# The feed-forward stages of a two-layer block multiply fp32 operands as they are

## The reference, cut to what matters

```
D_MODEL, SEQ, D_FF, CONV_WIDTH = 1024, 256, 2816, 3

def _conv_ffn(h, w_up, conv_w, conv_b, w_down):
    T = h.shape[1]
    u, v = jnp.split(h @ w_up, 2, axis=-1)
    up = jnp.pad(u, ((0, 0), (CONV_WIDTH - 1, 0), (0, 0)))
    uc = conv_b
    for j in range(CONV_WIDTH):
        uc = uc + up[:, j:j + T] * conv_w[j]
    return (jax.nn.silu(uc) * v) @ w_down

# in each layer of the first block:
        x = _layer_norm(ALPHA * x + g1 * y, ln_g[l, 0], ln_b[l, 0])
        h = x * (1.0 + sc2) + sh2
        y = _conv_ffn(h, ffn_w_up[l], ffn_conv_w[l], ffn_conv_b[l], ffn_w_down[l])
        x = _layer_norm(ALPHA * x + g2 * y, ln_g[l, 1], ln_b[l, 1])
```

## Time and profile before

| | us |
|---|---:|
| median of three runs | 4321.88 |
| the profiled execution | 4311.35 |
| its span, first to last instruction | 4309.5 |
| feed-forward part of layer 0, from its modulation to the next layer norm | 212.57 |
| feed-forward part of layer 1, likewise | 212.45 |
| TensorE busy in the whole span | 3165.2 (73%) |

### The profile page before, as it was taken

One profiled execution on the slowest core, in us unless ns is written; L12 is line 12 of the kernel. 1 busy time (PEld: TensorE's weight loads), 2 busy tenths in 40 slices (PEclk: granted clock), 3 DMA queues, 4 the chain that ended last, 5 costly groups with the idle time before them and its releaser, 6 DMA issues. The chain is left out here.

```text
span 4309.5 us, 38844 instructions
## 1 busy us (share of the span) xinstructions
PE 3165.2 (73%) x12396; PEld 1874.4 (43%) x12396; DVE 2309.2 (54%) x4812; ACT 1068.9 (25%) x2443; POOL 960.7 (22%) x820
## 2 busy tenths in 40 slices
PE   5767975987976877877776877777766654777776
PEld 1657934963834762322323432222254553322322
DVE  4456545746156358655554775555443658655554
ACT  1334422531232341111112211111132231111111
POOL 0000000000000032544443354444200013444442
PEclk9868997999986688999998999999987877999999
DMA  7214552545200127999996699999720024999996
GB/s 291 84 40 139 181 224 94 173 147 216 72 0 0 40 88 301 421 421 421 421 421 262 236 421 421 421 421 421 298 103 26 1 107 163 421 421 421 421 422 254
DMA packets 168918, 1062.44 MB, mean 247 GB/s; under 512 B 18604, under 2 KB 22444, under 8 KB 57664
## 3 DMA queue, kind: packets, MB, share of 16 engines
q0 software_dynamic: 110592, 805.36, 44.9%
q1 hardware_dynamic: 58176, 255.33, 16.4%
HBM read 1059.56 MB, written 1.05 MB: 246 GB/s over the span
## 5 line engine op out<-in xcount | busy, mean ns | idle before, releaser
L1775 PE MATMUL peer_fetch_summed<-peer_fetch_raw,peer_fetch_diag 128*128 128x512 f32 x3072 | 1440.2, 614 | 522.6 <-ACT peer_fetch_diag L1732 522.2
L1690 DVE CUSTOM_DVE_ANT_0 peer_fetch_raw<-peer_fetch_raw,peer_rows 128x1024 f32<-128x1024 f32 x768 | 940.4, 1225 | 873.8 <-DMA peer_fetch_raw<-in_peer_uv,peer_fetch_experts 873.5
L1775 PEld LDWEIGHTS peer_fetch_summed<-peer_fetch_raw,peer_fetch_diag 128*128 128x128 f32 x3072 | 563.4, 193 | 1395.5 <-ACT peer_fetch_diag L1732 820.6
L1612 POOL DMA_INDIRECT peer_fetch_raw<-in_peer_uv,peer_fetch_experts x768 | 846.2, 1102 | 1184.6 <-PE peer_fetch_summed L1775 1021.0
L1542 POOL TENSOR_TENSOR peer_keys_lo<-peer_pick_wq_raw,peer_keys_hi 128x1024 fp32r<-128x1024 f32 x48 | 114.3, 2386 | 2105.6 <-ACT peer_keys_hi L1501 2105.6
L1723 ACT ACTIVATE peer_fetch_gelu<-peer_fetch_score 128x2 f32<-128x2 f32 x384 | 78.1, 203 | 1605.2 <-DVE peer_fetch_score L1690 1605.2
L1732 ACT ACTIVATE peer_fetch_diag<-all_constants,peer_fetch_gelu 128x128 f32<-128x128 f32 x768 | 260.0, 386 | 0.3
L124 PE MATMUL ffn_up_acc<-first_h_hi,ffn_up_hi 128*128 128x256 f32 x704 | 201.4, 286 | 36.9 <-DVE ffn_up_lo L644 36.9
L124 PE MATMUL ffn_up_acc<-first_h_lo,ffn_up_hi 128*128 128x256 f32 x704 | 201.0, 286 | 0.0
L124 PE MATMUL ffn_up_acc<-first_h_hi,ffn_up_lo 128*128 128x256 f32 x704 | 200.9, 285 | 0.0
L452 PE MATMUL mod_acc<-mod_weights,mod_act_c 128*1 128x512 f32 (+1 forms) x288 | 135.6, 615 | 45.9 <-DMA mod_weights<-in_ada_w 32.3
(11 more groups left out here) (483 smaller groups left out, 4920.4 us busy)
## 6 DMA issues: line engine op xcount, KB each, us to landing
mod_weights<-in_ada_w SPq DMA_DIRECT2D x48, 1024.0 KB, 7.3
in_up_raw<-in_w_up SPq DMA_DIRECT2D x88, 512.0 KB, 4.1
mod_weights<-in_w_mod SPq DMA_DIRECT2D x24, 1024.0 KB, 6.4
peer_pick_wq_raw<-in_peer_wq SPq DMA_DIRECT2D x48, 512.0 KB, 3.2
peer_fetch_next_raw<-in_w_mod SPq DMA_DIRECT2D x24, 1024.0 KB, 4.8
ffn_down_raw<-in_w_down SPq DMA_DIRECT2D x32, 704.0 KB, 5.7
peer_fetch_raw<-in_peer_uv,peer_fetch_experts POOLq DMA_INDIRECT x768, 19.0
in_in_raw<-in_ab_w_in SPq DMA_DIRECT2D x17, 512.0 KB, 3.3
```

The costliest lines, as they stand in the source:

```text
L1612: nc.gpsimd.indirect_dma_start(raw[:, n % ring].rearrange("p c d -> p (c d)"), None, uv_rows, bass.IndirectOffsetOnAxis(index[:, i, e:e + ...
L1690: nc.vector.tensor_tensor_reduce(raw[:, n % ring, 0, :], raw[:, n % ring, 0, :], rows[:, i, :], 1.0, 0.0, ALU.mult, ALU.add, score[:, i, e ...
L1775: ins = nc.tensor.matmul(summed[:, i, half, :], diag[:, n % dring, :], raw[:, n % ring, 1, half * 512:(half + 1) * 512], start=(e == 0), s ...
```

## The change

In both feed-forward parts TensorE is given the fp32 operands themselves. The splitting and its buffers are gone from these parts; `pair` and `products` stay for the other stages.

- `scaled` takes the place of `modulate` ahead of these parts: `h` on VectorE, then `x` times ALPHA, with no parts, nothing on ScalarE, and no fetch of weights.
- `conv_ffn` is one stage and one block. SP fetches all 44 up chunks into a ring of 6 and all 16 down pieces into a ring of 4. TensorE makes 8 matmuls for an up chunk and 22 for a down chunk, straight from the ring, with three pairs of accumulators for up and two for down. The down matmuls follow the up matmuls on TensorE with no stage between them; the first half of them waits for 11 hidden chunks, the second for 22.
- The loops are written out by Python, with no loop of the engines.
- The stage around both (`in01`, `in11`), which held the early fetch, is gone.

The diff, cut to its core:

```diff
+def scaled(nc, name, h, x, mods, shift):
+
+    with Stage(nc, name) as st:
+        s_h = st.sem("h")
+        with nc.Block() as block:
+            @block.vector
+            def _(dve):
+                for k in range(KD):
+                    nc.vector.tensor_scalar(h[:, k, :], x[:, k, :], mods[:, shift + KD + k, 0:1], mods[:, shift + k, 0:1],
+                                            ALU.mult, ALU.add).then_inc(s_h, 1)
+                dve.wait_ge(s_h, KD)
+                nc.vector.tensor_scalar(x[:], x[:], ALPHA, None, ALU.mult)
...
-def conv_ffn(nc, name, pair, up_ahead, conv, w_down, z, gate):
...
-                    def body(m, slot, turn):
-                        pe.wait_ge(s_lo, m + 1)
-                        pe.wait_ge(s_taken, m + 1)
                         for k in range(KD):
-                            ins = products(nc, acc[:, slot, 0:T], part(w, slice(None), slot, slice(k * P, (k + 1) * P)),
-                                           part(pair, slice(None), k), start=(k == 0), stop=(k == KD - 1))
...
-        project(nc, name + "_down", down_ahead, KF, hidden_pair, T, [(KD, gate_to(nc, z, gate))])
+def conv_ffn(nc, name, h, w_up, conv, w_down, z, gate):
+    with Stage(nc, name) as st:
+        RING, BANKS, DOWN = 6, 3, 4
+        half = KF // 2
+        raw, down = st.sb("raw", [P, RING, KD * P]), st.sb("down", [P, DOWN, half * P])
+        hidden = st.sb("hidden", [P, KF, T])
+        ubuf, cbuf, sbuf = st.sb("u", [P, 2, T + 2]), st.sb("c", [P, 2, T]), st.sb("s", [P, 2, T])
+        acc = st.ps("acc", [P, BANKS, 2, 512])
+        out = st.ps("out", [P, 2, 512])
+        s_raw = [st.sem(f"raw{r}") for r in range(RING)]
+        s_down = [st.sem(f"down{r}") for r in range(DOWN)]
+        s_zero, s_up, s_u, s_tap, s_silu, s_hidden, s_part, s_taken = (
+            st.sem(n) for n in ("zero", "up", "u", "tap", "silu", "hidden", "part", "taken"))
+        with nc.Block() as block:
+            @block.sync
+            def _(sp):
+                def fetch_down(n):
+                    if n >= DOWN:
+                        sp.wait_ge(s_part, n - DOWN + 1)
+                    sp.dma_start(down[:, n % DOWN, :], w_down[n // 2, :, n % 2 * half * P:(n % 2 + 1) * half * P]).then_inc(s_down[n % DOWN], 16)
+                for m in range(2 * KF):
+                    if m >= RING:
+                        sp.wait_ge(s_up, m - RING + 1)
+                    sp.dma_start(raw[:, m % RING, :], w_up[m]).then_inc(s_raw[m % RING], 16)
+                for n in range(2 * KD):
+                    fetch_down(n)
+            @block.tensor
+            def _(pe):
+                for f in range(KF):
+                    if f >= BANKS:
+                        pe.wait_ge(s_u, f - BANKS + 1)
+                        pe.wait_ge(s_hidden, f - BANKS + 1)
+                    for i in range(2):
+                        m = 2 * f + i
+                        pe.wait_ge(s_raw[m % RING], 16 * (m // RING + 1))
                         for k in range(KD):
+                            ins = nc.tensor.matmul(acc[:, f % BANKS, i, 0:T], raw[:, m % RING, k * P:(k + 1) * P], h[:, k, :],
+                                                   start=(k == 0), stop=(k == KD - 1))
+                        ins.then_inc(s_up, 1)
+                for m in range(KD):
+                    if m >= 2:
+                        pe.wait_ge(s_taken, m - 1)
+                    for i in range(2):
+                        n = 2 * m + i
+                        pe.wait_ge(s_down[n % DOWN], 16 * (n // DOWN + 1))
+                        if m == 0:
+                            pe.wait_ge(s_hidden, (i + 1) * half)
+                        for k in range(half):
+                            ins = nc.tensor.matmul(out[:, m % 2, 0:T], down[:, n % DOWN, k * P:(k + 1) * P], hidden[:, i * half + k, :],
+                                                   start=(i == 0 and k == 0), stop=(i == 1 and k == half - 1))
+                        ins.then_inc(s_part, 1)
+            @block.scalar
+            def _(act):
+                act.wait_ge(s_zero, 1)
+                for f in range(KF + 1):
+                    if f < KF:
+                        act.wait_ge(s_up, 2 * f + 1)
+                        if f >= 2:
+                            act.wait_ge(s_tap, 3 * (f - 1))
+                        nc.scalar.activation(ubuf[:, f % 2, 2:2 + T], acc[:, f % BANKS, 0, 0:T], ACT.Copy).then_inc(s_u, 1)
+                    if f >= 1:
+                        act.wait_ge(s_tap, 3 * f)
+                        if f >= 3:
+                            act.wait_ge(s_hidden, f - 2)
+                        nc.scalar.activation(sbuf[:, (f - 1) % 2, :], cbuf[:, (f - 1) % 2, :], ACT.Silu).then_inc(s_silu, 1)
+                for m in range(KD):
+                    act.wait_ge(s_part, 2 * m + 2)
+                    nc.scalar.activation(z[:, m, :], out[:, m % 2, 0:T], ACT.Copy, scale=gate[:, m, :]).then_inc(s_taken, 1)
+            @block.vector
+            def _(dve):
+                nc.vector.memset(ubuf[:], 0.0).then_inc(s_zero, 1)
+                def taps(f):
+                    b = f % 2
+                    dve.wait_ge(s_u, f + 1)
+                    if f >= 2:
+                        dve.wait_ge(s_silu, f - 1)
+                    nc.vector.tensor_scalar(cbuf[:, b, :], ubuf[:, b, 0:T], conv[:, f, 0:1], conv[:, f, 3:4], ALU.mult, ALU.add).then_inc(s_tap, 1)
+                    for j in (1, 2):
+                        dve.wait_ge(s_tap, 3 * f + j)
+                        nc.vector.scalar_tensor_tensor(cbuf[:, b, :], ubuf[:, b, j:j + T], conv[:, f, j:j + 1], cbuf[:, b, :],
+                                                       ALU.mult, ALU.add).then_inc(s_tap, 1)
+                def gated(f):
+                    dve.wait_ge(s_silu, f + 1)
+                    dve.wait_ge(s_up, 2 * f + 2)
+                    nc.vector.tensor_tensor(hidden[:, f, :], sbuf[:, f % 2, :], acc[:, f % BANKS, 1, 0:T], ALU.mult).then_inc(s_hidden, 1)
+                taps(0)
+                for f in range(1, KF):
+                    taps(f)
+                    gated(f - 1)
+                gated(KF - 1)
...
         layer_norm(nc, "ln00", x, z, h, T, *ln(0, 0), con("mean_of_d"))
-        with Stage(nc, "in01") as st:
-            ahead = Ahead(nc, st, "up", d["w_up"][0])
-            modulate(nc, "h01", h, pair, x, mods, 3 * KD, (0,), ahead)
-            conv_ffn(nc, "ffn0", pair, ahead, conv(0), d["w_down"][0], z, mods[:, 5 * KD:, :])
+        scaled(nc, "h01", h, x, mods, 3 * KD)
+        conv_ffn(nc, "ffn0", h, d["w_up"][0], conv(0), d["w_down"][0], z, mods[:, 5 * KD:, :])
         layer_norm(nc, "ln01", x, z, h, T, *ln(0, 1), con("mean_of_d"))
...
```

More of the change, by code:

```diff
@@ L1844, in first_block @@
         layer_norm(nc, "ln10", x, z, h, T, *ln(1, 0), con("mean_of_d"), residual=False)
-        with Stage(nc, "in11") as st:
-            ahead = Ahead(nc, st, "up", d["w_up"][1])
-            modulate(nc, "h11", h, pair, x, mods, 3 * KD, (0,), ahead)
-            conv_ffn(nc, "ffn1", pair, ahead, conv(1), d["w_down"][1], z, mods[:, 5 * KD:, :])
+        scaled(nc, "h11", h, x, mods, 3 * KD)
+        conv_ffn(nc, "ffn1", h, d["w_up"][1], conv(1), d["w_down"][1], z, mods[:, 5 * KD:, :])
         layer_norm(nc, "ln11", x, z, h, T, *ln(1, 1), con("mean_of_d"))
```

95 lines of the change are left out of this document (removed).

## The result

| | before | after |
|---|---:|---:|
| median, first timing (4 runs each) | 4319.70 | 4367.36 |
| lowest and highest | 4314.00, 4322.67 | 4358.22, 4373.29 |
| the profiled execution | 4311.35 | 4369.84 |
| its span | 4309.5 | 4368.1 |
| layer 0's part | 212.57 | 239.79 |

The kernel became slower: the ratio is 1.011, 95% interval 1.0088 to 1.0132. The forecast was 4377.5 us in 4362 to 4392; the time lies in it, 10 us under the forecast itself. The forecast for the two parts was 55.7 us more; in the traces it is 27.22 + 27.65 = 54.9 us.

The account below looks back on a forecast made before the run. TensorE was taken to bound both feed-forward parts. Each part's terms summed to 240.3 us against 212.57 and 212.45, adding 55.7 us; profiled execution 4367.0, plus 10.5 for the median, gave 4377.5 us, range 4362 to 4392.

Parts of the forecast that it names:

- 1. `scaled`: Start of each part: eight instructions, a short wait and ALPHA take 3.99 us; the low parts (2.77 us) go.
- 2. the stage: Leaving the modulation's stage, before the next stage's first instruction: 0.84 us.
- 3. The first weights: Ahead of TensorE: the first weight fetch lies open, 3.6 us (ends 3.1 and 5.1); TensorE starts 8.4 us in.
- 4. 528 products in two passes: Up and down matmuls of a part: 1056 passes at 0.216 us, 228.1 us; a product 0.432 instead of 0.360.
- 5. The cold start: TensorE's first passes in a part at clock 0.50: 2.3 us lost, ends 1.5 and 3.3.
- 6. Up to down: Between up and down matmuls: no cost, where TensorE stood 5.56 us before and then ran cold again.
- 7. The end: After the last product: last pass runs out, ScalarE's copy, then one stage at 0.84 us; together 1.51 us.
- Two steps of the prediction that go beyond the parts: Whole program: median taken 10.5 us above the profiled execution's 4367.0; the parts' 55.7 us counted fully as the program's.
- halved rate for FP32_LOW_HIGH: Rival, all products of both parts: one pass each at 0.216 us, a part 126.3 us, program 4149 us; chance 0.04.
- the other two rivals: TensorE in the parts: clock falls under fp32 passes (4422 to 4822 us), or pauses between pieces (4414); chance 0.04 each.

Follow-up runs that it names:

- the run again: The changed kernel timed once more with no edit, against the kernel before: 4372.53 us, ratio 1.0145.
- the dear product alone: Kernel before, with one fp32 matmul of the high copy kept as fp32 in place of three F32R matmuls: 4392.91 us, ratio 1.0177.
- the early fetch: Changed kernel with the first six up chunks issued in the modulation's stage: 4377.94 us, ratio 1.0143 against the kernel before.

## Why the prediction was right

1. `scaled` and 2. the stage: 3.94 + 0.84 us against 3.99 + 0.84.
3. The first weights: 3.50 us against 3.6, issued 0.2 us before the first VectorE instruction; TensorE began 8.09 and 8.10 us in, against 8.4. In the run again 9.70 us occurred once: the bounds were needed.
4. 528 products in two passes: 1056 x 0.2158 = 227.9 us against 228.1. This is the step that decides, and the dear product alone in the old structure gave the same price. The steps of before, 0.1199 and 0.1195, were read 0.0003 and 0.0006 us too small, since the window also counts the matmul that it cuts; so the losses at the cold starts of before were read some 0.2 to 0.3 us too large.
5. The cold start: TensorE busy 230.37 and 230.67 less 227.9 and one record's overhang of 0.16 leaves 2.3 and 2.6 us, against 2.3.
6. Up to down: no idle time, no second cold start, as said.
7. The end: 1.33 us from TensorE's last end against 1.35.

The sum was 240.3 us a part; it is 239.79 and 240.10. The mechanism is thus right term by term, with errors of under 0.4 us in each.

The whole time was 4367.36 in the first timing and 4372.53 in the second, the forecast 4377.5. Two steps of the prediction that go beyond the parts were weaker than the sum. First, the prediction took the profiled execution of before as 10.5 us under the median and added that; the changed kernel's was 2.5 us over its own median, so this offset did not repeat, and the profiled execution (4369.84 against 4367.0) was met more closely than the median. Second, it said that what the parts gain or lose the program gains or loses. The layer norm behind layer 0's part took 17.88 us before and 16.19 now, since its first matmuls ran at 0.66 then and at 1.00 now; and the rest of the program moves by more than that from one execution to the next (last section). The range was wide enough for both.

The Trainium skill's halved rate for FP32_LOW_HIGH ("Perfetto Trace Analysis", "Engine Utilization"; an estimate of 0.213 us a product) stays contradicted: 0.432 us over 1056 products. No window inside the parts showed a low clock after the start, and there was no pause at any of the 60 pieces, so the other two rivals fell too.

## What to carry to other kernels

Where one engine is busy from end to end, count its passes and not its instructions: an fp32 matmul here is two passes of 0.216 us for 256 columns, three F32R matmuls are 0.360, and the work taken off engines that were hidden behind it was worth nothing. A change can hold a loss and a gain: joining two stages was worth 9 us a part, and undoing the dear half of the change while keeping its structure gave a kernel faster than both. To judge effects of some microseconds, read the stage that they are in, and the one behind it, which may start at another clock; the whole time may move by more for another reason.

## What the runs showed of the hardware that was not expected

One untouched stage of the second block, the window attention, takes from 95 to 114 us in the same code. These windows run over it in the profiled execution of before and of the changed kernel once more:

```profile
1352.80:1467.00 114.20, 112.36 (x400) 92.15 (x400) 39.80 (x120) 36.26 (x101) 0.00 (x0) 0.50 0.00 1
```
```profile
1411.00:1506.20 95.20, 88.97 (x400) 72.82 (x400) 39.81 (x120) 36.29 (x101) 0.00 (x0) 0.66 0.00 1
```

VectorE and ScalarE work the same time in both. What differs is the granted clock: 0.50 throughout in the one, 0.66 in the mean in the other. Of ten traces seven show 113.8 to 114.2 us from its first matmul to its last, two 94.7 and 94.8, one 109.6. That is 19 us, more than the error of the forecast, and a part of the spread between executions. It is not all of it: the early fetch's trace has 109.6 us here, 4 less than the changed kernel's, and is still 8 us longer as a whole, by small differences in many stages. What makes the clock rise in one execution and not in the next was not tried.

The F32R pass of 256 columns steps at 0.120 us, while an fp32 pass of 128 columns steps at 0.112. The Trainium skill ("TensorE: Matmul & The Clock Gate", "Back-to-back issue gap") gives N / 2.4 + 2.5 ns as the gap of a matmul taken by itself at the full clock. With two cycles a column, which the trace shows for an fp32 pass (0.427 us for 256 columns at 1.2 GHz), that estimate is 215.8 ns at 256 columns, and the trace has 215.8; at 128 columns it is 109.2 and the trace has 111.7. For F32R, at one cycle a column, it is 109.2 as well, and the trace has 120.

The kernel before also shows what kind of surplus that is. Its `gla_v` stage has F32R passes of 512 columns:

```profile
3245.00:3275.00 30.00, 30.00 (x134) 24.82 (x134) 3.68 (x3) 3.18 (x3) 0.00 (x0) 1.00 0.00 1
```

With one record's overhang of 0.389 us that is 0.227 us a pass. The columns alone, at 2.4 GHz, would be 0.2133 us, and 0.1067 at 256: the surplus is 13 ns at either length. At the low clock it isn't there: in the cold start of layer 0's part the F32R passes of 256 columns step at 0.214 us, and 256 columns at 1.2 GHz are 0.2133. So it goes with the pass and not with the columns, and only at the full clock. Its cause stays open; over the 1584 passes of a part it is some 20 us.
